# Moving three of the four result writes of the projections behind the page steps of a decoder layer

## The reference, cut to what matters

```python
def trunk_layer(x, p, pos, conv_left, attend, lw):
    h = x @ lw['w_in']
    cq, ckv, kr, conv_in, ga, gb = jnp.split(h, IN_OFFSETS, axis=-1)
    q = (rms_norm(cq, lw['q_norm_g']) @ lw['w_uq']).reshape(b, s, N_HEADS, QK_NOPE + QK_ROPE)
    c_kv = rms_norm(ckv, lw['kv_norm_g'])          # result 2: the latents, 520 rows of 256
    k_rope = rope(kr, pos)                         # result 3: the rotary keys, 520 rows of 32
    o_lat = attend(q_lat, q_rope, c_kv, k_rope)    # samples: over the pages and their own row
    branch_b = ...
    u = ca * jax.nn.sigmoid(cb)
    ext = jnp.concatenate([conv_left, u], axis=1)
    y = conv(ext)                                  # width 31, each channel by itself
    new_conv = ext[:, -CONV_STATE:]                # result 4: the last 30 rows (prompt, samples)
    branch_a = ...
    x = layer_norm(DN_ALPHA * x + mix, ...)
    ffn = hier_moe(x, ...)                         # 32 experts, two for each token
    ...
    return x, c_kv, k_rope, new_conv
```

## Time and profile before

| | |
|---|---|
| Median of three runs | 935.86 us (932.34 to 937.1) |
| The profiled execution | 934.52 us, its span 932.8 us |
| TensorE busy | 886.6 us, 95% of the span |
| VectorE, ScalarE, GpSimd busy | 482.7, 247.0, 146.0 us |
| Chain of work that ended last | TensorE 78%, transfers 12%, VectorE 5%, issue 2%, ScalarE 2% |
| Moved by transfers | 247.61 MB, mean 265 GB/s |
| SyncE's queue (q1), GpSimd's (q0), ScalarE's (q10) | 191.42, 35.29, 19.93 MB |

### The profile page before, as it was taken

One profiled execution on the slowest core, in us unless ns is written; L12 is line 12 of the kernel. 1 busy time (PEld: TensorE's weight loads), 2 busy tenths in 40 slices (PEclk: granted clock), 3 DMA queues, 4 the chain that ended last, 5 costly groups with the idle time before them and its releaser, 6 DMA issues.

```text
span 932.8 us, 14793 instructions
## 1 busy us (share of the span) xinstructions
PE 886.6 (95%) x5217; PEld 533.3 (57%) x5217; DVE 482.7 (52%) x1093; ACT 247.0 (26%) x553; POOL 146.0 (16%) x242
## 2 busy tenths in 40 slices
PE   8999999999999999999999999899999889888897
PEld 7777777777776766656678644443333333333343
DVE  2343789977752258677666346661111211114784
ACT  1122221112243125756620111221111111002246
POOL 0323433334334000000000000011211101111000
PEclk9999999999999999999999999999999989989999
DMA  9977998999999420101241595639999999998601
GB/s 373 372 254 247 337 340 279 332 369 309 320 333 329 169 75 20 49 20 43 113 191 47 212 427 242 237 120 407 425 421 423 424 420 426 422 418 343 236 24 69
DMA packets 76178, 247.61 MB, mean 265 GB/s; under 512 B 15397, under 2 KB 22830, under 8 KB 67110
## 3 DMA queue, kind: packets, MB, share of 16 engines
q1 hardware_dynamic: 54422, 191.42, 53.4%
q0 software_dynamic: 16288, 35.29, 10.6%
q10 hardware_dynamic: 5392, 19.93, 6.0%
HBM read 240.98 MB, written 18.05 MB: 278 GB/s over the span
## 4 chain that ended last, share of the span: by engine, by line
PE 78%; DMA 12%; DVE 5%; issue 2%; ACT 2%; SPq 0%; POOL 0%; DVEq 0%; ACTq 0%; POOLq 0%
PE ps L1068 12%; PE ps L1572 9%; PE ps L1019 8%; DMA arena<-in_wexp 8%; PE ps L1492 6%; PE ps L1594 4%; PE ps L1416 4%; PE ps L1127 3%; PE ps L1157 3%; PE ps L1242 3%; PE ps L1059 3%; PE ps L1697 2%; PE ps L1264 2%; DMA y_scratch<-arena,idy 2%; PE ps L1206 2%
## 5 line engine op out<-in xcount | busy, mean ns | idle before, releaser
L1068 PE MATMUL ps<-arena 128*128 128x260 f32 x544 | 125.9, 387 | 1.4 <-DMA arena<-in_xT 0.9
L1068 PEld LDWEIGHTS ps<-arena 128*128 128x128 f32 x544 | 101.8, 191 | 22.4 <-issue 4.5
L2118 DVE SCALAR_TENSOR_TENSOR arena<-arena,vec 128x512 f32<-128x512 f32 x120 | 81.8, 745 | 0.0
L1019 PE MATMUL ps<-arena 128*128 128x260 f32 x336 | 78.5, 387 | 0.1
L1572 PE MATMUL ps<-arena 128*64 128x512 f32 x288 | 66.8, 617 | 7.4 <-DMA arena<-in_wexp 6.4
L2989 POOL DMA_DIRECT2D arena<-in_kv x96 | 52.3, 546 | 134.7 <-issue 130.9
L2814 DVE TENSOR_TENSOR arena<-ps,arena 128x256 f32<-128x256 f32 x18 | 7.6, 425 | 126.9 <-ACT arena L1967 126.9
L1594 PE MATMUL ps<-arena 128*64 128x512 f32 x288 | 67.4, 610 | 4.2 <-DMA arena<-in_wexp 4.2
L1019 PEld LDWEIGHTS ps<-arena 128*128 128x128 f32 x336 | 62.1, 190 | 12.9 <-issue 3.2
L1572 PE MATMUL ps<-arena,con 128*64 128x512 f32 x288 | 63.8, 595 | 2.3 <-DMA arena<-in_wexp 2.3
L2996 POOL DMA_DIRECT2D arena<-in_kr x96 | 48.2, 502 | 63.8 <-issue 57.2
(11 more groups left out here) (424 smaller groups left out, 1356.4 us busy)
## 6 DMA issues: line engine op xcount, KB each, us to landing
arena<-in_wexp SPq DMA_DIRECT2D x26, 2048.0 KB, 24.0
arena<-in_kv SPq DMA_DIRECT2D x160, 256.0 KB, 8.8
arena<-in_wexp SPq DMA_DIRECT2D x36, 1024.0 KB, 27.2
arena<-in_kv POOLq DMA_DIRECT2D x96, 256.0 KB, 7.3
arena<-in_w ACTq DMA_DIRECT2D x35, 512.0 KB, 8.4
arena<-in_wexp SPq DMA_DIRECT2D x16, 512.0 KB, 4.7
arena<-in_wo SPq DMA_DIRECT2D x8, 512.0 KB, 4.6
arena<-in_w_out SPq DMA_DIRECT2D x4, 1024.0 KB, 7.3
```

The costliest lines, as they stand in the source:

```text
L1019: y = mm(ps[:, paired_bank(p, n), 0:TH], left(k), right(k), start=(k == 0), stop=(k == KD // 2 - 1))
L1068: y = mm(ps[:, b + h, 0:TH], w[:, k], xT[:, k, h * TH:(h + 1) * TH], start=(k == 0), stop=(k == KD - 1))
L2118: y = v.scalar_tensor_tensor(out=aT[:, c, 0:NPR], in0=win, scalar=wt, in1=aT[:, c, 0:NPR], op0=ALU.mult, op1=ALU.add)
```

## The change

The write `conv_p` stays in the turn n = 8. The other three (`conv_s`, the wait for `s_nrm`, `ckv`, `krope`) go behind the loop over the steps and behind the first two pairs' weights. ScalarE's wait before the squares asks for one write (16) in place of four (64); the two other waits for `s_out` keep their 64.

```diff
@@ -771,10 +771,6 @@
                 if n == 8:
                     sp.wait_ge(s_gl, 2 * KC)
                     sp.dma_start(o["conv_p"], ext[:, :, NPR:NPR + CW - 1]).then_inc(s_out, 16)
-                    sp.dma_start(o["conv_s"], exs[:]).then_inc(s_out, 16)
-                    sp.wait_ge(s_nrm, N_NRM)
-                    sp.dma_start(o["ckv"], hT[:, B_CKV:B_CKV + KKV, :]).then_inc(s_out, 16)
-                    sp.dma_start(o["krope"], hT[64:96, B_KR, :]).then_inc(s_out, 16)
                 sp.wait_ge(s_ks, n - 1)
                 step_keys(n)
                 sp.wait_ge(s_vs, n - 1)
@@ -783,6 +779,10 @@
             for s in range(2):
                 sp.dma_start(pw[:, s], a["wpair"][s]).then_inc(s_pw[s], 16)
                 sp.dma_start(wr[:, s], a["wrope"][s]).then_inc(s_rw[s], 16)
+            sp.dma_start(o["conv_s"], exs[:]).then_inc(s_out, 16)
+            sp.wait_ge(s_nrm, N_NRM)
+            sp.dma_start(o["ckv"], hT[:, B_CKV:B_CKV + KKV, :]).then_inc(s_out, 16)
+            sp.dma_start(o["krope"], hT[64:96, B_KR, :]).then_inc(s_out, 16)
 
             for p in range(2, PAIRS):
                 sp.wait_ge(s_gv, p - 1)
@@ -1821,7 +1821,7 @@
                 if (kind, j) == ("cs", 0):
 
-                    act.wait_ge(s_out, 64)
+                    act.wait_ge(s_out, 16)
                     for c in range(KC):
                         act.wait_ge(s_ln, 1 + c)
                         av(sqc(c), aT[:, c], ACT.Square).then_inc(s_sqc, 1)
```

## The result

The changed kernel took 929.44 us (median of 7 runs, 928.51 to 931.96) beside 934.95 us for the kernel before: a ratio of 0.9949 (0.9924 to 0.9974). Timed twice more beside the kernel before, it gave 0.9975 (0.9964 to 0.9987) and 0.9964 (0.9952 to 0.9977). The intervals overlap, so that the difference between the three need not be more than noise; their mean is 0.9963, 3.5 us of 935. The forecast of 3.0 us is 0.9968, inside all three intervals. The profiled execution gained more, 6.0 us (934.52 to 928.51). All ratios are of fast executions; four executions of 1029 to 3226 us (three of the kernel before, one of the kernel that moves conv_s alone) are left out of them.

The account below looks back on a forecast made before the run. TensorE was taken to bound the page stage, with four short transfer stalls. Gains of 0.3 + 1.28 + 1.4 = 3.0 us, moved writes costing 0, take the median from 935.86 to 932.9 us; range 929.5 to 936.6.

Parts of the forecast that it names:

- The sum: Page stage: gains of 0.3, 1.28 and 1.4 us at page steps 7, 8 and 9, together 3.0 us; chance 0.62.
- step 8: Page step 8: keys and pages issued 6.0 us earlier land by 192.7, so all of its 1.28 us stall goes.
- The signs named ahead: L1127 waits fall to two or three, step 8 pages issued near 174, last page step about 3 us earlier.
- step 7: Page step 7: pages queued before the writes, so only 0.3 of its 2.31 us stall goes.
- step 9: Page step 9: pages issued near 193.1, 1.4 us of its 1.75 us stall won, 0 to 0.6 stays.
- (A): Rival: the writes' bytes decide, all three stalls at page steps 7 to 9 go, gain 5.3 us; chance 0.18.
- the queue shields step 7: Page step 7: engines consume one queue in order, so pages ahead of the writes lose nothing; the sum would be 2.7.
- Step 14: Page step 14: its 2.11 us stall lies eighty us behind the writes and stays as it is, effect 0.
- Part 2 and 3: Writes behind the page stage fall into a transfer gap, and the changed waits on writes matter nowhere; cost 0 each.
- (B): Rival: the stalls come back at page steps 10 to 12, about 2.4 of 3.0 us, gain 0.6; chance 0.16.
- (C): Rival: writes run beside the pages of page step 15, TensorE waits 8.6 us there, profiled 940.1; chance 0.04.

Follow-up runs that it names:

- the delay alone: Changed kernel with SyncE also made to wait for the values of page step 6 before the keys of step 8, without the writes' bytes; ratio 0.9982.
- step 11: Kernel before with all four writes moved from ahead of the keys of page step 8 to ahead of those of page step 11; ratio 0.9962.
- step 15: Changed kernel with the three writes ahead of the keys of page step 15 instead of behind the page steps; ratio 0.9967.
- conv_p at 11: Changed kernel with the conv_p write moved from ahead of the keys of page step 8 to ahead of those of page step 11; ratio 0.9969.
- changed again: Changed kernel run a second time without any edit; ratio 0.9975 to the kernel before.

## Why the prediction was right, and where not

**The sum.** 3.0 us were forecast. Step 10 starts 3.4 to 3.6 us earlier, and the mean of the three timings is 3.5. In us, the forecast was 932.9 with a range of 929.5 to 936.6 around a kernel before of 935.86; the median of 929.44 lies at the low edge, beside a kernel before that was itself 0.9 faster (934.95). By the ratio it would be 935.86 x 0.9949 = 931.1. Of the terms behind the number that of step 8 came true; those of steps 7 and 9 missed in opposite directions in two of three profiles, and the reasoning of steps 8 and 9 failed, as told below. That the sum held is in part luck.

**The signs named ahead.** L1127's waits fell from four to three in the first profile (five and two in the others), and the last page step started 5.3, 1.3 and 5.6 us earlier (3 was forecast). Three signs did not come: the pages of step 8 were issued from 177.17 (and 178.10 and 176.47), not near 174; step 7 kept 1.43, 0.16 and 0.11, not about 2.0; step 9 kept up to 1.43, not at most 0.6.

**Steps 8 and 9.** Step 8 was to lose all of its stall and did. Step 9 was to keep 0 to 0.6 and kept 0, 1.36 and 1.43. The working behind these terms is the step that failed: it moved the landings back by as much as the issues. The pages of step 8 were to start 6.0 us earlier and to land by 192.7; they started 2.8 us earlier, because the ten key issues ahead of them took 8.44 us and not 4.91, and landed at 196.0 where they had landed at 198.6, 2.5 us earlier. The reserve that step 8 was given, 4.7 us or 2.4, was 0.9, and 0.3 in the two other profiles. The run with the delay alone shows that the start of the issues isn't what counts: its pages were issued from 180.05, as in the earlier trace rows, and the last landed at 195.5. What the transfer engines and the queue have to carry does: with 1.1 MB of writes in the queue the last page left later and landed at 198.6. The 2.9 us of full rate for these bytes, which the prediction worked out and used only for (A), is nearer to the mechanism than the 5.99 us of issue. That both gave a number near 3 hid this.

**Step 7.** 0.3 us were forecast to go and 0.9 went in the first profile, 2.1 and 2.2 in the two others. In these two the term was too small by 1.9, and the term of step 9 (1.4, measured 0.4 and 0.3) too large by 1.0 and 1.1. What one step gains the next can lose: the size that can be forecast is the stall of the three together, 5.2 to 1.5, not each (of these 3.7 us 0.3 come back at step 6, which stalls 0.35 where it stalled 0.06). That the queue shields step 7 was right in part: it took 6.98 us with the writes in another queue and 2.2 to 2.3 with them behind it, but 0.1 to 1.5 with none of the three.

**Step 14.** "Stay as they are: 0" was wrong for a single profile, which is where the gap between 6.0 us there and the timings comes from. The changed kernel has it at 0, 2.27 and 0. Whether it is scatter alone stays open: of the seven profiles with writes in SyncE's queue between pages (before twice, conv_s moved twice, the others moved, step 11, step 15) six stalled by 1.3 to 2.3 us there; of the six with none but conv_p (changed three times, delay, left out, conv_p at 11) one did. The means of the kernels before and changed are 2.1 and 0.8. If that is more than chance, some of the gain comes from there, by a way that no run here shows.

**Part 2 and 3.** Free, as forecast: leaving the writes out changes nothing, and the 6.0 us of issue, 3.8 in fact, had 30 us of cover.

**The rivals.** (A), all three stalls gone, didn't come: 1.5 us stay, and 1.3 of them with no write near. Its reason, that the bytes decide, is the one that the runs bear out; its size is not. (B), the stalls return at steps 10 to 13: 0.45, 0.27 and 0 at step 12. (C) didn't come. Its delay is real where the writes stand ahead of the pages of step 15 (3.0 us), but behind these pages it can't be: they landed at 308.9 in the changed kernel, before any of the writes (313.0 to 315.4).

Why steps 7 to 9 have no reserve and step 11 has one is only argued. ScalarE's queue in the kernel before, 160 to 200 us:

```profile
163.13 1.12 ACTq L1716 DMA_DIRECT2D arena<-in_w  x2
...
181.01 0.85 ACTq L1716 DMA_DIRECT2D arena<-in_w  x2
...
198.63 0.85 ACTq L1716 DMA_DIRECT2D arena<-in_w  x2
```

With the pages of each of these steps two weight blocks of 512 KB are under way at once; from 208 us on ScalarE issues one at a time, 9 to 14 us apart. The transfer engines' share was 1.03 from 160 to 212 us, and 0.88 from 230 to 250. No run moved the blocks, and from 285 to 310 the share is as high (1.04 in the kernel before), so that the share alone doesn't tell the two places apart.

## What to carry to other kernels

Where transfers and the engine that waits for them are both nearly full, ask of each transfer which steps it shares a queue and a stretch with, and whether these have reserve: 1.1 MB of writes cost 3.7 us of stall at one place, 0.9 and at most 1.9 us at two others of the same stage, and nothing that could be measured behind it. Do not split a stall over neighbouring steps more finely than over the stretch as a whole, and test a late issue by a delay without bytes before blaming it, up to the last issue and not only the first. If a write must go out beside an urgent read, put it behind the read in the same queue: here it cost in another queue, in one run, half as much again in stall and twice as much in time.

## What the runs showed of the hardware that was not expected

A stall of TensorE can cost more than itself. Behind 2.27 us of idle time (changed again, step 14) the granted clock was 0.60 for 3 us, which cost another 1.7 us; behind 6.98 us it was 0.60 for 5 us, and another 2.1 us went. Yet behind 2.31 us (before, step 7) and 2.33 us (conv_s moved again, step 14) the same 32 products took 1.93 us, about the full clock's time. What decides between these is not shown here; it makes single profiles of this kernel differ by 4 us in one stall, and three intervals, not one profile, were needed for the size.

To start a step's pages earlier need not land them earlier. The last page of step 8 landed at 196.0 when the ten left from 177.17, and at 195.5 when they left from 180.05; the ten key issues ahead of them took 8.44 us in the first case and 4.90 in the second.
